# A recurrent block's first RMSNorm, folded behind its first GEMMs: the normaliser applied on the way out of PSUM

## The reference

```python
def rmsnorm_2(x, g):
    xf = x.astype(jnp.float32)
    y = xf * lax.rsqrt(jnp.mean(xf * xf, axis=-1, keepdims=True) + EPS)
    return (y * g.astype(jnp.float32)).astype(x.dtype)
...
        h = rmsnorm_2(x, norm_mix[l])
        qa, ka, va, za, alpha, beta, qb, kb, vb, ga, gb = _split_cols(h @ w_in[l], IN_SPLITS)
        qkv = jax.nn.silu(_causal_dwconv(jnp.concatenate([qa, ka, va], axis=-1), conv_w[l]))
        qa, ka, va = _split_cols(qkv, (A_QK, A_QK, A_VW))
        oa = _gated_deltanet(qa, ka, va, alpha, beta, a_log[l], dt_bias[l])
```

## Time and profile before

| | us |
|---|---|
| median of 3 runs (2514.92 to 2517.38) | 2515.11 |
| the profiled execution, its own time | 2515.88 |
| its span in the profile | 2514.1 |
| PE busy | 2329.7 (93%) |
| DVE busy | 998.1 (40%) |
| ACT busy | 811.5 (32%) |
| POOL busy | 818.3 (33%) |
| mean granted clock of PE | 0.965 |

### The profile page before, as it was taken

The page is one execution under the profiler, slowest core; times in us unless marked ns, Lnnn a source line. Parts: engine busy times, 40 slices in busy tenths (PEclk is TensorE's granted clock), DMA queues, the critical chain, the costliest instruction groups (busy, mean ns, idle before and its releaser), DMA issues.

```text
span 2514.1 us, 29045 instructions
## 1 busy us (share of the span) xinstructions
PE 2329.7 (93%) x11804; PEld 1874.0 (75%) x11804; DVE 998.1 (40%) x1609; ACT 811.5 (32%) x1184; POOL 818.3 (33%) x234
## 2 busy tenths in 40 slices
PE   7758999989999979989898999999899899999998
PEld 3535788867888868878787788667588788788887
DVE  3685623142111246564636320533536345322202
ACT  3333532223222325242424222333423343222212
POOL 0746323433344423020211133122133332344342
PEclk9877999989999989999999999999999899999999
DMA  6412122222332222010101023112123231223321
GB/s 233 134 50 84 51 78 84 93 92 67 101 100 89 95 88 75 26 51 18 51 18 51 17 84 109 51 43 88 46 77 108 79 123 64 81 90 100 100 98 53
DMA packets 178610, 197.47 MB, mean 79 GB/s; under 512 B 3412, under 2 KB 170816, under 8 KB 178496
## 3 DMA queue, kind: packets, MB, share of 16 engines
q1 hardware_dynamic: 176848, 190.84, 23.6%
q10 hardware_dynamic: 1648, 5.02, 0.5%
HBM read 193.76 MB, written 2.10 MB: 78 GB/s over the span
## 4 chain that ended last, share of the span: by engine, by line
PE 81%; DVE 6%; issue 2%; ACT 2%; POOL 1%; DMA 0%; ACTq 0%; DVEq 0%; POOLq 0%
PE ps L1824 20%; PE ps L1826 19%; PE ps L1825 19%; PE ps L2120 3%; PE ps L1924 3%; PE ps L2086 2%; PE ps L2324 1%; PE ps L2315 1%; PE ps L2082 1%; PE ps L2322 1%; POOL w_lo L599 1%; PE ps L1918 1%; PE ps L1871 1%; PE ps L1873 1%; PE ps L1872 1%
## 5 line engine op out<-in xcount | busy, mean ns | idle before, releaser
L599 POOL TENSOR_TENSOR w_lo<-raw,w_hi 128x2048 fp32r<-128x2048 f32 (+1 forms) x150 | 681.1, 4541 | 1485.9 <-ACT w_hi L673 1485.9
L1824 PE MATMUL ps<-h_hi,w_hi 128*128 128x512 f32 x1384 | 561.4, 406 | 21.6 <-POOL w_lo L599 6.0
L1826 PE MATMUL ps<-h_hi,w_lo 128*128 128x512 f32 x1384 | 544.9, 394 | 0.0
L1825 PE MATMUL ps<-h_lo,w_hi 128*128 128x512 f32 x1384 | 544.1, 393 | 0.0
L673 ACT ACTIVATE w_hi<-raw 128x2048 fp32r<-128x2048 f32 x150 | 285.6, 1904 | 395.7 <-PE ps L1826 394.6
L1824 PEld LDWEIGHTS ps<-h_hi,w_hi 128*128 128x128 f32 x1384 | 263.3, 190 | 101.5 <-issue 39.2
L1826 PEld LDWEIGHTS ps<-h_hi,w_lo 128*128 128x128 f32 x1384 | 262.7, 190 | 57.4
L1825 PEld LDWEIGHTS ps<-h_lo,w_hi 128*128 128x128 f32 x1384 | 263.7, 191 | 50.1
L1824 PE MATMUL ps<-g_hi,w_hi 128*128 128x512 f32 x256 | 100.9, 394 | 0.0
L1826 PE MATMUL ps<-g_hi,w_lo 128*128 128x512 f32 x256 | 100.4, 392 | 0.0
L1825 PE MATMUL ps<-g_lo,w_hi 128*128 128x512 f32 x256 | 99.4, 388 | 0.0
(11 more groups left out here) (370 smaller groups left out, 4052.1 us busy)
## 6 DMA issues: line engine op xcount, KB each, us to landing
raw<-w_in SPq DMA_DIRECT2D x48, 1024.0 KB, 5.2
raw<-w_down SPq DMA_DIRECT2D x27, 1024.0 KB, 5.1
raw<-ada_w SPq DMA_DIRECT2D x24, 1024.0 KB, 5.2
raw<-w_gate_up SPq DMA_DIRECT2D x22, 1024.0 KB, 5.1
raw<-w_up SPq DMA_DIRECT2D x16, 1024.0 KB, 5.5
raw<-w_mkv SPq DMA_DIRECT2D x8, 1024.0 KB, 5.6
raw<-w_out SPq DMA_DIRECT2D x4, 1024.0 KB, 5.2
raw<-w_a_out SPq DMA_DIRECT2D x4, 1024.0 KB, 5.2
```

What stands on the lines that cost most here:

```text
L599: nc.gpsimd.tensor_tensor(w_lo[:, split_at[u] % 2, 0:n], raw[:, u % 2, 0:n], w_hi[:, split_at[u] % 2, 0:n].bitcast(F32), ALU.subtract).the ...
L1824: T.matmul(out_, wh, hi, start=start, stop=False, skip_group_check=True)
L1825: T.matmul(out_, wh, lo, start=False, stop=False, skip_group_check=True)
L1826: return T.matmul(out_, wl, hi, start=False, stop=stop, skip_group_check=True)
```

## The change

- The gain is multiplied into the stream without the reciprocal while the last MLP chunk runs: ACT makes h_hi = round(xT * gain) for each tile just ahead of the square, DVE makes h_lo (`mix_lower`) just ahead of `add_square`.
- PE runs the GEMM of unit ab on these tiles before `norm_sum`, and the GEMM of unit pair0 in eight pieces (`piece`: six matmuls for one k) after it, with `spread` between the second and the third piece.
- ACT copies the spread reciprocal to acc (`keep_spread`); this is one more increment of rb_done, so three later waits count one higher. DVE multiplies it in when it stores ab_T and, later, the two query tiles to pad_in; ACT stored these before.
- h_hi and h_lo are then made anew, normalised, in the same buffers: `normed` and `norm_hi` as before, but tile k's `norm_hi` waits until PE has run piece k (mix_piece; for the last one tile_done).
- The GEMM of unit pair0+1 comes next, each k waiting for the normalised h_lo; the turn of ab_T stands behind it, the GEMM of pair0+2 behind that, then the gates' sums, then pair0+3.
- On ACT the w_hi of pair0+1 is made right after `std_of`, that of pair0+2 right after `norm_hi`; `pair_qkv(0, 0)` is gone, so the w_hi of pair0+3, in `pair_qkv(0, 1)`, stands behind the wait for gate_dve 3.

```diff
@@ scalar (ACT)
                     for jj in range(2 if last else 0):
                         act.wait_ge(bank_stored[bank_of(u0_ + 4 + j, jj)], stored_count(u0_ + 4 + j, jj))
-                        squares(N_MIX, 2 * j + jj, xT[:, 2 * j + jj, :])
+                        k = 2 * j + jj
+                        nc.scalar.activation(h_hi[:, k, :], xT[:, k, :], ACT.Copy,
+                                             scale=col("norm_mix_2", k)).then_inc(sem["mix_hi"], 1)
+                        squares(N_MIX, k, xT[:, k, :])
...
             std_of(N_MIX, 1.0 / D)
-            norm_hi(N_MIX, h_hi, None)
-
-
-            store_tile(first["ab"], 0, ab_T[:, :], rows=16)
             next_hi()
+            keep_spread(N_MIX, acc[:, :])
+            for k in range(KT):
+                if k < KT - 1:
+                    act.wait_ge(sem["mix_piece"], k + 1)
+                else:
+                    act.wait_ge(sem["tile_done"], tile_count(first["pair0"], 1))
+                norm_hi(N_MIX, h_hi, None, [k])
+            next_hi()
...
                     act.wait_ge(sem["c_pad"], 1)
-                    pair_qkv(p, 0)
                     act.wait_ge(sem["gate_dve"], 3)
@@ vector (DVE)
+            def mix_lower(k):
+
+                dve.wait_ge(sem["mix_hi"], k + 1)
+                V.scalar_tensor_tensor(h_lo[:, k, :], xT[:, k, :], col("norm_mix_2", k), h_hi[:, k, :].bitcast(F32),
+                                       ALU.mult, ALU.subtract).then_inc(sem["mix_lo"], 1)
...
                         if last and k:
+                            mix_lower(k - 1)
                             add_square(N_MIX, k - 1)
...
+            mix_lower(KT - 1)
             add_square(N_MIX, KT - 1)
             inverse_of(N_MIX)
+            u = first["ab"]
+            dve.wait_ge(sem["rb_done"], 1)
+            dve.wait_ge(sem["tile_done"], tile_count(u, 0))
+            V.tensor_tensor(ab_T[:, :], bank(u, 0)[0:16, :], acc[0:16, :], ALU.mult).then_inc(bank_stored[bank_of(u, 0)], 1)
             normed(N_MIX, xT, lambda k: col("norm_mix_2", k), h_lo, h_hi, None)
+            V.memset(pad_in[:, :, 0:3], 0.0).then_inc(sem["c_pad"], 1)
+            u = first["pair0"]
+            for a in range(2):
+                dve.wait_ge(sem["tile_done"], tile_count(u, a))
+                V.tensor_tensor(pad_in[:, a, 3:3 + S], bank(u, a), acc[:, :], ALU.mult).then_inc(bank_stored[bank_of(u, a)], 1)
...
@@ tensor (PE)
+            u = first["ab"]
+            gemm(u, [([(k * P, h_hi[:, k, :], h_lo[:, k, :]) for k in range(KT)], S)], ready=after(sem["mix_lo"], 0))
             norm_sum(N_MIX)
-            spread(N_MIX)
-
-
-            u = first["ab"]
-            gemm(u, [([(k * P, h_hi[:, k, :], h_lo[:, k, :]) for k in range(KT)], S)], ready=after(sem["n_lo"], 24))
+            for k in range(KT):
+                if k == 2:
+                    spread(N_MIX)
+                ins = piece(first["pair0"], k)
+                if k < KT - 1:
+                    ins.then_inc(sem["mix_piece"], 1)
+            wide_gemm(first["pair0"] + 1, h_hi, h_lo, ready=after(sem["n_lo"], 24))
             pe.wait_ge(bank_stored[bank_of(u, 0)], stored_count(u, 0))
             for tt in range(NT):
                 ins = turn(ps[:, 4, tt * 16:(tt + 1) * 16], ab_T[:, tt * P:(tt + 1) * P])
             ins.then_inc(sem["ab_turned"], 1)
-            wide_gemm(first["pair0"], h_hi, h_lo)
+            wide_gemm(first["pair0"] + 2, h_hi, h_lo)
             pe.wait_ge(sem["gate_dve"], 2)
...
                 if p == 0:
-                    for kind in range(1, 4):
-                        wide_gemm(u + kind, h_hi, h_lo)
+                    wide_gemm(u + 3, h_hi, h_lo)
```

More of the change, by code:

```diff
@@ L405, in build @@
     y_lo_done g_lo_done ab_turned gate_cum c_normed kv_turned k_scaled qd_done kk_mm nL_done inv0_done lv_mm
-    lv_done r_init r_ws r_u r_st o_scaled o_turned oa_lo_done rb_done gate_silu gate_scaled s_lo_done""".split()
+    lv_done r_init r_ws r_u r_st o_scaled o_turned oa_lo_done rb_done mix_hi mix_lo mix_piece gate_silu gate_scaled s_lo_done""".split()
     sem = {n: nc.alloc_semaphore(n) for n in names}
@@ L1543, in _ @@
             mlp_chunk(first["mlp"] + 24, 24, last=True)
+            mix_lower(KT - 1)
             add_square(N_MIX, KT - 1)
             inverse_of(N_MIX)
+            u = first["ab"]
+            dve.wait_ge(sem["rb_done"], 1)
+            dve.wait_ge(sem["tile_done"], tile_count(u, 0))
+            V.tensor_tensor(ab_T[:, :], bank(u, 0)[0:16, :], acc[0:16, :], ALU.mult).then_inc(bank_stored[bank_of(u, 0)], 1)
             normed(N_MIX, xT, lambda k: col("norm_mix_2", k), h_lo, h_hi, None)
+            V.memset(pad_in[:, :, 0:3], 0.0).then_inc(sem["c_pad"], 1)
[3 more added lines that the diff above has]
+                V.tensor_tensor(pad_in[:, a, 3:3 + S], bank(u, a), acc[:, :], ALU.mult).then_inc(bank_stored[bank_of(u, a)], 1)
             ab = ps[:, 4, 0:NT * 16].rearrange("p (t c) -> p t c", c=16)
             dve.wait_ge(sem["ab_turned"], 1)
-            V.memset(pad_in[:, :, 0:3], 0.0).then_inc(sem["c_pad"], 1)
             V.tensor_tensor(gp[:, 0, :, :], ab[:, :, 0:HA], bc[:, 2 * QK1:2 * QK1 + HA].unsqueeze(1).broadcast_to([P, NT, HA]),
@@ L1745, in memory_query @@
                 u, jj = first["mq"] + k // 2, k % 2
-                dve.wait_ge(sem["rb_done"], 1)
+                dve.wait_ge(sem["rb_done"], 2)
                 dve.wait_ge(sem["tile_done"], tile_count(u, jj))
@@ L1774, in gu_round @@
                 if loop is None:
-                    dve.wait_ge(sem["rb_done"], 2)
+                    dve.wait_ge(sem["rb_done"], 3)
                 for jj in range(2):
@@ L1893, in piece @@
                         ins.then_inc(sem["tile_done"], 1)
+                return ins
             def after(done, base):
@@ L2420, in _ @@
             pe.wait_ge(sem["m_in_done"], 16)
-            pe.wait_ge(sem["rb_done"], 1)
+            pe.wait_ge(sem["rb_done"], 2)
             turn_memory(range(4))
@@ L2480, in _ @@
                 pe.wait_ge(bank_stored[bank_of(first["gu"] + 21, j)], stored_count(first["gu"] + 21, j))
-            pe.wait_ge(sem["rb_done"], 2)
+            pe.wait_ge(sem["rb_done"], 3)
             down(0)
```

## The result

The change makes the kernel slower. Over 11 timed runs the median is 2522.61 us (2519.3 to 2529.68), beside 2517.38 us (2511.43 to 2520.67) for the kernel before in the same rounds; the ratio over the rounds is 1.0027, 95% interval 1.0016 to 1.0038, some 6.8 us (the two medians by themselves are 5.2 us apart). The forecast was +4.7 us, which it held to be just under what a measurement can tell, with no change as the likeliest of the three outcomes. The interval excludes no change: the order of events was right, the size was too small. A profile of the changed kernel shows a span of 2523.3 us against 2514.1 us, +9.2 us, for an execution of 2525.12 us, which lies 2.5 us above its kernel's median.

The account below looks back on a forecast made before the run. Two chains bound it within 0.4 us: PE's GEMMs, and gates, convolutions, SiLU, root, the second setting the time. Root +2.7 and norm clock +2.0 gave +4.7 us, 2519.8 us for the median; range 2512 to 2523.5.

Parts of the forecast that it names:

- PE resumes with tile 6: Unit ab's GEMM after the MLP: PE waits 3.2 us for tile 6, until 924.3.
- The lead at the front: PE after the MLP: pair0 begins some 14 us sooner, although gate_dve 3 comes 8.7 us later.
- the queue behind gate_dve 3 on ACT: Exponentials, keys' stores and the w_hi of pair0+3 follow that wait, so POOL gets the w_hi at 967.4.
- the wait of z: PE, ready for the z GEMM (pair0+3) at 964.0, waits 8 us for POOL's w_lo.
- two stops in the convolutions back to back: DVE's convolutions stand still during two consecutive POOL subtractions, 967.4 to 976.6; cost taken as 8.5 us.
- the exposed root: Norm of q and k: the root starts 2.7 us later, at 991.75, PE having stood still for 5 us.
- the two clock terms: Low PE clock after the wait for tile 6 and in the q and k norm; each taken as 2.0 us.
- the two gaps of the earlier trace: PE gaps of 3.18 and 3.31 us, old pace back 3.4 and 5.0 us later; used to price low clock.
- The second: Norm of q and k: PE restarts at low clock after standing still 5 us; 2.0 us lost.
- the likeliest case: Whole kernel: +4.7 us, bounds +3.1 to +7.6, chance 0.60, split 0.35 same and 0.25 slower.
- The first: Front of PE: low clock after the wait for tile 6 of unit ab; 2.0 us lost.
- the rival that had 0.17: Low clock through the whole q and k norm: some 5.5 us instead of 2.0, +8.1, 2523.2; chance 0.17.

Follow-up runs that it names:

- e1: Changed kernel with the key tiles' stores and the w_hi of pair0+3 moved ahead of the gates on ACT; ratio to the kernel before 1.0007.
- e2: Changed kernel with the two query-tile convolutions run on DVE right after the tiles are stored, before the gates; ratio to the kernel before 0.9994.
- e3: Changed kernel with the turn of ab_T and the gate sums each one GEMM earlier on PE; ratio to the kernel before 0.9997.
- e10: Changed kernel with the w_hi of pair1+0, and so its POOL subtraction, moved behind the convolutions; ratio to the kernel before 1.0011.
- e4: Changed kernel with 18 unused matmuls of constants on PE behind its second sum of squares; ratio to the kernel before 1.0019.
- e5: Changed kernel with unused matmuls in both PE waits: 18 behind the second sum of squares, 12 before tile 6 of ab; ratio to before 0.9991.
- e7: Changed kernel with the orders on PE, ACT and DVE all rearranged (gate sums, keys' stores, convolutions earlier); ratio to the kernel before 0.9979.
- e6: One part of the change: unit ab on the unnormalised operand, query GEMM on normalised tiles, ACT and DVE ordered as before; ratio to before 0.9998.
- e11: The changed kernel unaltered, profiled and timed a second time; ratio to the kernel before 1.0031.
- e9: The kernel before with 30 unused matmuls of constants on PE in its wait ahead of norm_sum; ratio to the kernel before 1.0003.
- e8: Changed kernel with PE, ACT and DVE orders all rearranged, plus 12 unused matmuls in each of PE's two waits; ratio to the kernel before 0.9943.

## Why the prediction was right in its order and wrong in its size

Times are again after the MLP's end; the forecast's are its own less 917.0.

| step | forecast | measured |
|---|---|---|
| PE resumes with tile 6 | 7.3 | 7.3 |
| gate_dve 3 | 47.0 | 48.6 |
| wait of pair0+3 for w_lo | 8 | 8.35 |
| convolutions begin | 47.65 | 49.2 |
| stops in them | 8.5 | 4.25 + 4.19 = 8.4 |
| last convolution ends | 72.8 | 74.3 |
| root, against before | +2.7 | +4.2 |
| root to turn, against before | +2.0 | +4.8 |
| turn, against before | +4.7 | +9.0 |

**What held.** The lead at the front, the queue behind gate_dve 3 on ACT, the wait of z, L1567's counterpart free of a stop (0.19 us at 966.64), two stops in the convolutions back to back, the exposed root, and nothing given back later. e1 (PE's stream is not what counts), e2 (the convolutions are), e3 (the gates' place on PE is why they start late) and e10 (POOL stops them) each show one link.

**The steps that failed** are the two clock terms, both taken as 2.0 us from the two gaps of the earlier trace rows, and measured as 3.4 and 4.8 us. With them failed the outcome held likeliest, no change. The rows were also read roughly: half of 3.4 and 5.0 us is 1.7 to 2.5, not 1.5 to 2.6, and behind the second gap the first 1.4 us still ran at the full pace (eight turns in 1.09 us), so that the two gaps cost 1.6 us (eight matmuls in 3.42 us instead of 1.82) and 1.7 us (eleven in 4.19 instead of 2.51). The low level lasted some 3.3 us behind each; in the changed kernel it lasted 6.8 us at the front and 10.6 in the norm.

The second is the worse. I let PE return to the full level within 3 to 5 us of its wait, as it had in a GEMM. In the norm of q and k it did not return at all until the turn: 11.9 us from root to turn against 7.1, 4.8 us lost instead of 2.0. e4 shows the whole term to be clock. The text had this case as a rival, with a price of +5.5 us, and gave it 0.17; the row to rank it by was there, the mean clock of 0.74 in the stretch with the same short instructions. It should have been the likeliest case, as the rows of a GEMM say little of a stretch of one-column sums and spreads.

The first was 3.4 us in this profile, from 926.7 to 933.5 us at half pace, instead of 2.0; e5, with that wait filled, gives 2.9 to 3.2 us for it. It isn't the same in each execution: full clock in e3 and e7, low in the changed kernel, e1, e2, e4, e6, e10 and e11, after one and the same wait of 3.14 or 3.15 us.

With the measured terms in place the working gives 4.7 + 1.4 + 2.8 = +8.9 us, the profile's +9.0; e11's is +8.4. That 2522.61 us lies in the forecast range, and +6.8 us in the +3.1 to +7.6 of the likeliest case, is no credit to the working: in both profiles the turn is later than this case allows, by the mechanism of the rival that had 0.17. Of the 2.8 us between 2519.8 and 2522.61 the kernel before was itself 2.3 us slower in these rounds than in the three runs that the forecast built on.

Why the ratio says 6.8 and not 9 is answered in part by which executions were profiled. The changed kernel's lay 2.5 us above its median and the kernel before's 1.5 us under 2517.38; without both, 9.2 us become 5.2. The record shows that the clock goes with it: of 27 timed runs of the kernel before, the ten quickest (2511.03 to 2513.97 us) have a mean granted clock of 0.964 to 0.967 and the ten slowest (2518.25 to 2520.18) one of 0.960 to 0.963, and the slowest of 11 of the changed kernel (2529.68) has 0.957. Where in such a run the clock was low is not seen. That the norm of q and k is one such place is: in e9, whose GEMMs end without a gap as in the kernel before, its second half ran at the low level, 10.3 us from root to turn against 7.1.

The Trainium skill's port rule (SBUF — State Buffer, "SBUF: two separate sides") agrees with the stop of L1605, which has two SBUF inputs (4.94 us against 0.75); the stop of L1604 and the only one of e10 hit an instruction with one tensor input, which the rule as the prediction gave it does not cover. The Trainium skill's drain after a table load (ScalarE: Activation LUTs, "What ACT_TABLE_LOAD costs") again didn't show: load at 992.52, 1.28 us, root at 993.82.

## What to carry to other kernels

When work is moved ahead on the busiest engine, write down for each other engine what now stands behind which wait: here the gates moved behind one GEMM more, and a weight's rounding behind the gates, and a lead of 14 us at the front ended as a loss. A gain of a stream is a gain only once every chain that meets it has been moved along; none of the single moves gave a gain clear of none, all three queues together did (0.9979). And a new wait of some microseconds on TensorE is to be priced with the slow matmuls behind it, by rows of the same kind of work, the short instructions above all.

## What the runs showed of the hardware that I had not expected

- TensorE's granted clock fell to the lower level in the middle of the q and k norm with no wait ahead of it: in e9 the first spread and sum took 1.14 and 0.95 us, the next 1.91 and 1.71 us, and the GEMMs before them had run without a break; e6 shows the same. It doesn't in each execution: the kernel before and e2 kept the full level there without a filling. In the three profiles with 12 or 18 matmuls of constants put in (e8; e4 and e5) the norm stayed at full pace.
- After the same wait of 3.14 or 3.15 us behind a full-speed GEMM the clock fell in seven profiles and not in two others (norm_sum 1.67 to 1.70 us, or 0.95 us). Where it fell, the first matmul behind the wait still took 0.50 us, as at the full level.
- Between two POOL subtractions back to back DVE got exactly one instruction through: 4.73 us for one that takes 0.48, then 4.94 us for one that takes 0.75. The first of them has one tensor input, so such an instruction stood still too.
- ACT loads a table ahead of the wait of the instruction that needs it. In the changed kernel:

```profile
948.92 1.28 ACT L986 ACT_TABLE_LOAD   x1
954.56 0.23 ACT L986 ACTIVATE gp<-gp 128x32 f32<-128x32 f32 x1 [4.35 <-DVE gp L1578]
```

The load ran at 948.92, 5.6 us before its activation, in time that would have been idle.
